# Throw-away products on TensorE in the routing's wait and ahead of three pairs of heads, and the number of expert rounds found ahead of the gates

## The chip, the cores and the metric

One core of one Trainium2 chip runs the whole program. The metric is the device time of one execution in microseconds (us). TensorE is called PE below, VectorE DVE, ScalarE ACT, GpSimd POOL and SyncE SP. SP and POOL issue the transfers (DMAs) from the chip's memory (HBM).

## What is computed

Two model blocks are run one after the other on 256 tokens of width 1024. The first block has a retention mixer, a recurrent mixer and two feed-forward networks. The second has a state-space mixer in both directions of time with a Fourier mixer beside it, and then a mixture of experts. The change touches two places in the second block.

```python
# state-space mixer, one pass (forward or backward): 16 heads, chunks of 128 tokens
seg    = where(lower, a_lr[..., :, None] - a_lr[..., None, :], -inf)
cb     = einsum('bclgn,bcsgn->bcgls', cm, bm)
y_diag = einsum('bcgrls,bcsgrp->bclgrp', cb[:, :, :, None] * exp(seg), xd)
y_off  = einsum('bcqgn,bcgrpn->bcqgrp', cm, h_in) * exp(a_cs)[..., None]
...
# hierarchical mixture of experts: 4 groups of 8 experts, the 2 best of the best group
p_grp = softmax(t @ w_rg + b_rg);  p_top_grp, grp = top_k(p_grp, 1)
p_exp = softmax(logit_sel);        p_top, j_top = top_k(p_exp, 2)
gate  = p_top_grp * p_top / sum(p_top)
y     = sum over a token's two experts of gate * ((silu(x @ w_eg) * (x @ w_eu)) @ w_ed)
```

## The kernel before

The program is one instruction stream for each engine, written by hand, with semaphores between them. An engine works strictly in the order of its stream, so a wait holds everything behind it.

**Weights.** They come from HBM in units of 128 partitions x 4096 numbers (2 MB) into six ring slots. SP issues the loads and waits for a slot to be released by PE (`slot_used`). The expert weights are 96 units, six for each pair of experts (gate, up and down, two halves each), so 16 pairs are worked off one after the other. Half of a gate unit of pairs 1, 10 and 13 is loaded into other tiles ("held": `cst`, `act2`, `lr2`, `spare`, `SQ`, `HM`, `work`), each when the tile has become free. The last held parts go into the first columns of `work`, where the routing keeps its scratch data (line 531 and the two `hold` calls behind it): SP waits there, and the loads of all later expert units are behind this wait in SP's stream.

**Heads of the state-space mixer.** The 16 heads are done in eight pairs. `head_order()` gives PE's order: for pair i first a `cb` product where a new group of four heads begins, then the `row` products of heads 2i+4 and 2i+5 (two pairs ahead), then `y`, the pair itself. Every `cb`, `row` and `y` result is a tile in one of six PSUM banks taken in turn (`ROT`), so a tile waits with `await_room` until the tile six places before it has been read. By this turn `y` of pair 1 takes the bank of row 4, `y` of pair 3 that of row 8, and `y` of pair 7 that of `y` 4. For each head h ACT reads `row` h (four activations into `HM`, or on odd heads DVE clamps it there), takes an exponential of the row into `act2` (this is the read that frees the bank) and one of `HM`, DVE multiplies `HM` with the masked `cb` (`m_ready`), and POOL multiplies `act2` with C (`ce_ready`). `y` of pair i waits for both of its heads. The tiles `HM` have four places, so head h waits for `y` of pair h/2-2. DVE also does `y_out` of each pair. After pair 7 comes the output product `mix_out`, whose last release lets SP load further expert units.

PE's stream at a pair:

```python
t = TILE["y", i]
await_room(pe, t)
...
pe.wait_ge(s["m_ready"], 2 * i + 2)
pe.wait_ge(s["ce_ready"], 2 * i + 2)
```

**Routing.** PE forms logits and turns the tokens; DVE picks group and experts in many small instructions and writes the selection `msk`. PE waits for it, counts each token's place in its expert's list (tile `route` 1, with `upper` and `ones`), counts the experts' totals into the bank `STAT` (`count_full`), and then gathers the tokens of the first experts (`gather`, 32 products into `xg` by way of ACT). DVE meanwhile makes positions, the selection `S2`, the low parts of the tokens (`token_rest`), the gates, and last the number of rounds (more than one round is needed only when an expert has over 64 tokens). `route_ready` tells all engines that the number stands in `rounds`; PE, ACT and DVE then load it into a register and enter the expert loop. `sel_ready` follows when DVE has made `SGb`, its last use of the routing's scratch.

Of the kernel before, what the change touches and what calls it, by code (L numbers as in the profile page):

```python
# [35 lines left out]
ALU = mybir.AluOpType  # L36
# [3 lines left out]
P = 128  # L40
T = 256
# [25 lines left out]
NE = NG * NJ  # L67
KE = FE // P
CAP = 64
# [156 lines left out]
def two_blocks(nc, a, out):  # L226

    ctx = ExitStack()
    with ctx:
# [242 lines left out]
        @block.sync  # L472
        def _(sp):
            sp.dma_start(vec[:, :], a["vec"]).then_inc(s["ld_vec"], 16)
            for j, piece in enumerate(("x", "w", "x", "w", "x", "x", "w", "w")):
                if piece == "x":
                    n = (0, None, 1, None, 2, 3)[j]
                    sp.dma_start(X[:, 2 * n:2 * n + 2, :], a["x"][:, 2 * n:2 * n + 2, :]).then_inc(x_in[n], 16)
                else:
                    n = (None, 0, None, 1, None, None, 2, 3)[j]  # L480
                    part = slice(n * CHUNK, (n + 1) * CHUNK)
                    sp.dma_start(ring[0][:, part], a["dense"][0][:, part]).then_inc(first_in[n], 16)
            for u in range(1, DENSE):
                if TURN[u]:
                    sp.wait_ge(slot_used[SLOT[u]], TURN[u])
                if u == DENSE - 1:
                    await_full(sp, TILE["state", SG_ - 1])
                sp.dma_start(ring[SLOT[u]][:, :], a["dense"][u]).then_inc(slot_full[SLOT[u]], 16)

            def load_expert(n, unit):  # L490
                i = EXPERT_SLOT[n]
                sp.dma_start(ring[i][:, :], a["experts"][bass.ds(unit, 1)].rearrange("u p n -> (u p) n")).then_inc(
                    slot_full[i], 16)

            def slot_free(k, r, turn):

                back = r * ring_uses(k) + turn
                sp.wait_ge(slot_used[EXPERT_SLOT[k]], back + (DENSE_USES[EXPERT_SLOT[k]] + (k == LAST_PLACE)))

            def expert_rest(r):  # L500
                with sp.Fori(0, EXPERT_UNITS // RING - 2) as b:
                    for k in range(RING):
                        slot_free(k, r, b + 1)
                        load_expert(k, b * RING + k + RING + HELD)
                for k in range(RING - HELD):
                    slot_free(k, r, EXPERT_UNITS // RING - 1)
                    load_expert(k, EXPERT_UNITS - RING + k + HELD)

            def hold(n, x, first):
                part = a["experts"][RING + n][:, first * FE:first * FE + x.shape[1]]  # L510
                sp.dma_start(x, part).then_inc(held_in[n], 16)

            hold(1, spare[:, :], 0)
            for n in range(RING):
                if EXPERT_SLOT[n] == PART_SLOT:
                    sp.wait_ge(s["h_ready"], KD)
                    first = 0
                    for x in (flat_cst, act2[:, :, :].rearrange("p a b -> p (a b)"), lr2[:, :, :].rearrange("p a b -> p (a b)")):
                        part = a["experts"][RING][:, first:first + x.shape[1]]
                        sp.dma_start(x, part).then_inc(held_in[0], 16)  # L520
                        first += x.shape[1]
                    sp.wait_ge(s["chunk_used"], CHUNKS)
                else:
                    if EXPERT_SLOT[n] == FOUR_SLOT:
                        sp.wait_ge(s["chunk_used"], MIX0 + FG)
                    sp.wait_ge(slot_used[EXPERT_SLOT[n]], DENSE_USES[EXPERT_SLOT[n]])
                load_expert(n, n)
            sp.wait_ge(s["rtok_full"], 2)
            hold(2, flat_sq[:, 0:4 * FE], 0)
            hold(2, flat_hm[:, 2 * FE:4 * FE], 4)  # L530
            sp.wait_ge(s["route_ready"], 1)
            hold(2, work[:, 0:2 * FE], 6)
            hold(1, work[:, 2 * FE:4 * FE], 6)
            expert_rest(0)
            n_rounds = sp.value_load(rounds[0:1, 0:1], min_val=1, max_val=T // CAP)
            with sp.If(n_rounds > 1):
                with sp.Fori(1, n_rounds) as r:
                    for n in range(RING):
                        slot_free(n, r, 0)
                        load_expert(n, n)  # L540
                    expert_rest(r)
            for j in range(4):
                sp.wait_ge(s["last_dve"], j + 1)
                sp.dma_start(out[:, 2 * j:2 * j + 2, :], H[:, 2 * j:2 * j + 2, :]).then_inc(s["out_done"], 16)
            sp.wait_ge(s["out_done"], 64)
# [72 lines left out]
        def _(pe):  # L618
# [285 lines left out]
            mod_rows(10)  # L904
            mod_rows(11)

            def release(name, i):
                left.append(slot_used[SLOT[UNIT_AT[name, i]]])

# [167 lines left out]
            for kind, i in head_order():  # L1077
# [10 lines left out]
                elif kind == "row":  # L1088
                    t = TILE["row", i]
                    await_room(pe, t)  # L1090
                    for d in range(2):
                        n = d * SH + i
                        one = one_of[:, n:n + 1].to_broadcast([ND, P])
                        mm(bank(t)[:, d * T:(d + 1) * T], one, a_hi[:, :], True, False)
                        mm(bank(t)[:, d * T:(d + 1) * T], one, a_lo[:, :], False, True,
                           bank_full[t % ROT] if d == 1 else None)
                else:
                    t = TILE["y", i]
                    await_room(pe, t)
                    if i == 0:  # L1100
                        pe.wait_ge(s["xd_ready"], 4)
                        await_read(pe, TILE["state", 2])
                        await_read(pe, TILE["state", 3])
                    pe.wait_ge(s["m_ready"], 2 * i + 2)
                    pe.wait_ge(s["ce_ready"], 2 * i + 2)
                    for part in range(6):
                        for h in (2 * i, 2 * i + 1):
                            rows, lo = slice(h % 2 * SP_, (h % 2 + 1) * SP_), h % 4 * SP_
                            head = slice(h * SP_, (h + 1) * SP_)
                            dm, state_of = decm[:, h % 4, :], h0[:, h // 4, :]  # L1110
                            x, cols, y = (
                                (xf[:, 0, head], slice(0, T), dm[:, 0:T]),
                                (xb[:, 0, head], slice(0, P), dm[:, T:T + P]),
                                (xf[:, 1, head], slice(P, T), dm[:, 384:384 + P]),
                                (xb[:, 1, head], slice(0, T), dm[:, 384 + P:768]),
                                (state_of[:, lo:lo + SP_], slice(0, T), ce_at[h % 4][:, 0:T]),
                                (state_of[:, 256 + lo:256 + lo + SP_], slice(0, T), ce_at[h % 4][:, T:2 * T]))[part]
                            mm(bank(t)[rows, cols], x, y, part == 0, part == 5,
                               bank_full[t % ROT] if part == 5 and h % 2 else None)
                    if i % 2 and i > 1:  # L1120
                        y_sums(i // 2 - 1)
# [54 lines left out]
                    turned(tt, [X[:, 4 * half + c, tau * P:(tau + 1) * P] for c in range(4)])  # L1176
            t = TILE["route", 1]
            await_room(pe, t)
            pe.wait_ge(s["msk_ready"], 1)
            mm(bank(t)[:, 0:NE], upper[:, :], msk[:, 0, :], True, True)  # L1180
            mm(bank(t)[:, NE:2 * NE], ones[:, :], msk[:, 0, :], True, False)
# [671 lines left out]
        def _(dve):  # L1853
# [617 lines left out]
            tt(cut(S2[:, 0, :, :].rearrange("p a b -> p (a b)"), 8, CAP), iota8, whole(posP, 0), EQ, s["eq_ready"])  # L2471
            token_rest(2)
            token_rest(3)
            dve.wait_ge(s["exp_ready"], 2)
            settle(reduce(r2(12), r2n(1, NG), ADD))
            settle(ts(r2(15), r2(14), 1.0, ADD))
# [7 lines left out]
                i = tt(cut(gw[:, tau, :], NG, NJ), og[:, tau, :].unsqueeze(2).to_broadcast([P, NG, NJ]),  # L2484
                       r2n(21, NJ)[:, tau:tau + 1, :].to_broadcast([P, NG, NJ]), MUL)
            settle(i)
            dve.wait_ge(s["count_full"], 1)
            settle(reduce(rt[:, 22, 0:1], ps[:, STAT, T:T + NE], MAX))
            for tau in range(2):
                i = ts(gP[:, tau], cut(gw[:, tau, :], NE // 4, 4), 1.0, MUL)  # L2490
            settle(i)
            ts(posP[:, NE // 4, :], posP[:, 0, :], float(CAP), SUB)
            settle(dve.tensor_copy(gateP[:, NE // 4, :], gateP[:, 0, :]))
            settle(ts(rt[:, 22, 1:2], rt[:, 22, 0:1], float(CAP), ALU.is_gt, 1.0, ADD))
            for n in range(2, T // CAP):
                settle(stt(rt[:, 22, 1:2], rt[:, 22, 0:1], float(CAP * n), rt[:, 22, 1:2], ALU.is_gt, ADD))
            dve.tensor_copy(rounds[:, 0:1], rt[:, 22, 1:2]).then_inc(s["route_ready"], 1)
            dve.wait_ge(s["route_ready"], 1)
            ts(rt[:, 23, 0:1], rt[:, 22, 0:1], 1.0, MUL, inc=s["moe_init"])
            dve.wait_ge(s["eq_ready"], 1)  # L2500
            tt(cut(SGb[:, 0, :, :].rearrange("p a b -> p (a b)"), 8, CAP),
               cut(S2[:, 0, :, :].rearrange("p a b -> p (a b)"), 8, CAP).bitcast(F32), whole(gateP, 0), MUL, s["sel_ready"])
# [224 lines left out]
```

## Time and profile before

| | |
|---|---|
| median of 3 runs | 1483.33 us (1483.03 to 1485.86) |
| the profiled execution | 1487.35 us, of which span of instructions 1485.6 us |
| PE busy | 1419.5 us (96%) |
| DVE busy | 821.1 us (55%) |
| ACT busy | 622.1 us (42%) |
| mean granted TensorE clock | 0.990 |
| transfers | 383.22 MB |

The span is the time from the first to the last instruction; 1.75 us of the profiled execution lie around it. A busy PE isn't PE at its peak, since its instructions overlap. A granted clock of 1.00 is 2.4 GHz, one of 0.50 is 1.2 GHz. In the last third of the span the transfers are nearly always busy.

### The profile page before, as it was taken

Reading aid. Unit: us, or ns where it says so; the run is one execution under the profiler, and the core shown is the slowest. Engines: PE = TensorE matmul, PEld = TensorE weight load, DVE = VectorE, ACT = ScalarE, POOL = GpSimd, SP = SyncE. Lnnn points to the kernel's source line nnn. Section 1 sums busy time; section 2 is a strip of 40 time slices with the busy share of each in tenths; the row PEclk is TensorE's granted clock in tenths of the full one; section 3 lists DMA queues with packets and bytes.
Section 4 is the critical chain, followed back from the end, with each engine's and each line's share of the span. In section 5 each row is a group of like instructions: output and inputs, shape, how many; then the busy total and the mean of one; then the engine's idle time right before and its main releaser. Section 6 shows DMA issues by size and latency. Waiting matters only on the chain.

```text
span 1485.6 us, 23733 instructions
## 1 busy us (share of the span) xinstructions
PE 1419.5 (96%) x9884; PEld 1122.0 (76%) x9884; DVE 821.1 (55%) x1216; ACT 622.1 (42%) x899; POOL 85.0 (6%) x65
## 2 busy tenths in 40 slices
PE   7999999999999999999999999798999999999997
PEld 7989799999989888999999998596434443434434
DVE  5557847776468578777458886954222222222223
ACT  6554345443456656545456665643111111111112
POOL 2000000000003102020010001500000000000000
PEclk9999999999999999999999999899999999999999
DMA  9654347445574566445561051247999999999994
GB/s 378 237 199 170 114 171 312 170 171 193 203 285 171 225 251 260 171 170 186 202 240 63 32 227 38 119 164 311 419 422 427 428 429 427 429 427 427 428 427 194
DMA packets 29041, 383.22 MB, mean 258 GB/s; under 512 B 3296, under 2 KB 3424, under 8 KB 5776
## 3 DMA queue, kind: packets, MB, share of 16 engines
q1 hardware_dynamic: 28224, 377.71, 62.7%
q0 software_dynamic: 720, 4.11, 0.7%
q8 instruction: 74, 1.21, 0.3%
q14 instruction: 23, 0.19, 0.0%
HBM read 380.76 MB, written 1.05 MB: 257 GB/s over the span
## 4 chain that ended last, share of the span: by engine, by line
PE 75%; DVE 10%; DMA 7%; ACT 5%; issue 2%; POOL 0%; SPq 0%; DVEq 0%; ACTq 0%; POOLq 0%
PE ps L631 74%; DMA ring<-in_experts 7%; DVE w_lo L1863 3%; ACT work L1334 2%; DVE work L1875 2%; ACT w_hi L1334 1%; DVE work L1863 1%; DVE X L1875 1%; ACT HM L1334 1%; DVE HM L1863 1%; DVE act L1863 0%; ACT L1334 0%; ACT act L1334 0%; PE ps L1286 0%; DMA ring<-in_dense 0%
## 5 line engine op out<-in xcount | busy, mean ns | idle before, releaser
L1863 DVE TENSOR_TENSOR w_lo<-ring,w_hi 128x1024 fp32r<-128x1024 f32 x272 | 339.7, 1258 | 215.9 <-ACT w_hi L1334 215.6
L631 PE MATMUL ps<-in_hi,w_hi 128*128 128x256 f32 x1376 | 392.8, 285 | 14.7 <-DVE w_lo L1863 14.3
L631 PE MATMUL ps<-in_hi,w_lo 128*128 128x256 f32 x1376 | 389.2, 283 | 0.0
L631 PE MATMUL ps<-in_lo,w_hi 128*128 128x256 f32 x1376 | 388.8, 283 | 0.0
L1334 ACT ACTIVATE w_hi<-ring 128x1024 fp32r<-128x1024 f32 x272 | 286.0, 1055 | 240.0 <-PE ps L631 235.9
L631 PE MATMUL ps<-ring,work 128*64 128x512 f32 (+2 forms) x1552 | 336.1, 582 | 16.2 <-ACT work L1334 12.4
L631 PEld LDWEIGHTS ps<-in_hi,w_hi 128*128 128x128 f32 x1376 | 261.7, 190 | 19.6 <-issue 16.9
L631 PEld LDWEIGHTS ps<-ring,work 128*64 128x64 f32 (+1 forms) x1552 | 113.0, 138 | 216.1 <-issue 195.8
L631 PEld LDWEIGHTS ps<-in_lo,w_hi 128*128 128x128 f32 x1376 | 261.8, 190 | 0.2
L631 PEld LDWEIGHTS ps<-in_hi,w_lo 128*128 128x128 f32 x1376 | 261.7, 190 | 0.0
L1334 ACT ACTIVATE work<-ps 128x512 f32<-128x512 f32 x64 | 37.7, 594 | 316.5 <-PE ps L1286 193.1
L1875 DVE SCALAR_TENSOR_TENSOR X<-ps,mod,X 128x256 f32<-128x256 f32 x136 | 56.8, 478 | 90.2 <-PE ps L631 89.3
L1875 DVE SCALAR_TENSOR_TENSOR yp_lo<-ps,small,yp_hi 128x512 fp32r<-128x512 f32 (+1 forms) x34 | 24.4, 719 | 147.9 <-ACT yp_hi L1334 146.5
L631 PE MATMUL ps<-hid_hi,w_hi 128*128 128x256 f32 x352 | 99.3, 282 | 0.0
L631 PE MATMUL ps<-hid_hi,w_lo 128*128 128x256 f32 x352 | 99.3, 282 | 0.0
L631 PE MATMUL ps<-hid_lo,w_hi 128*128 128x256 f32 x352 | 99.1, 282 | 0.0
L1863 DVE TENSOR_TENSOR work<-work,ps 128x512 f32<-128x512 f32 x24 | 16.1, 684 | 105.1 <-PE ps L631 105.1
L631 PEld LDWEIGHTS ps<-hid_lo,w_hi 128*128 128x128 f32 x352 | 66.7, 189 | 0.0
L631 PEld LDWEIGHTS ps<-hid_hi,w_hi 128*128 128x128 f32 x352 | 66.7, 189 | 0.0
L631 PEld LDWEIGHTS ps<-hid_hi,w_lo 128*128 128x128 f32 x352 | 66.7, 189 | 0.0
L1334 ACT ACTIVATE yp_hi<-ps,small 128x512 fp32r<-128x512 f32 (+1 forms) x34 | 22.5, 662 | 77.7 <-PE ps L631 77.7
L1875 DVE SCALAR_TENSOR_TENSOR work<-ps,vec,work 128x254 f32<-128x254 f32 (+3 forms) x80 | 44.7, 585 | 11.8 <-ACT work L1334 10.4
(283 smaller groups left out, 2053.6 us busy)
## 6 DMA issues: line engine op xcount, KB each, us to landing
ring<-in_experts SPq DMA_DIRECT2D x93, 2048.0 KB, 20.5
ring<-in_dense SPq DMA_DIRECT2D x82, 2048.0 KB, 8.5
ring<-in_dense SPq DMA_DIRECT2D x4, 512.0 KB, 7.5
spare<-in_experts SPq DMA_DIRECT2D x1, 1536.0 KB, 11.4
cst<-in_ret_cst POOLq DMA_DIRECT2D x1, 1280.0 KB, 13.1
cst<-in_experts SPq DMA_DIRECT2D x1, 1280.0 KB, 11.1
X<-in_x SPq DMA_DIRECT2D x4, 256.0 KB, 6.5
cst<-in_ctx POOLq DMA_DIRECT2D x1, 1024.0 KB, 7.8
```

What stands on the lines that cost most here:

```text
L631: i = pe.matmul(o, l, r, start=start, stop=stop)
L1334: x = act.activation(o, i, f, **kw)
L1863: i = dve.tensor_tensor(out=o, in0=x, in1=y, op=op)
L1875: i = dve.scalar_tensor_tensor(out=o, in0=x, scalar=sc, in1=y, op0=op0, op1=op1)
```

## The change

`keep_clock(n)` issues n products of `ones` with `ones` (128x128 numbers, fp32) into a bank that nobody reads. PE does 6 of them ahead of pair 1, 9 ahead of pair 3 and 8 ahead of pair 7, behind `await_room` and ahead of the waits for `m_ready` and `ce_ready`; and 16 ahead of the wait for `msk` in the routing. DVE finds the number of rounds directly behind `token_rest(3)`, ahead of the gates. SP waits for `sel_ready` where it waited for `route_ready`.

```diff
@@ block.sync
             hold(2, flat_hm[:, 2 * FE:4 * FE], 4)
-            sp.wait_ge(s["route_ready"], 1)
+            sp.wait_ge(s["sel_ready"], 1)
             hold(2, work[:, 0:2 * FE], 6)
             hold(1, work[:, 2 * FE:4 * FE], 6)
             expert_rest(0)
@@ block.tensor
+            def keep_clock(n):
+
+                for _ in range(n):
+                    pe.matmul(ps[:, MODB, 0:P], ones[:, :], ones[:, :], start=True, stop=True)
+
...
                         await_read(pe, TILE["state", 2])
                         await_read(pe, TILE["state", 3])
+                    keep_clock({1: 6, 3: 9, 7: 8}.get(i, 0))
                     pe.wait_ge(s["m_ready"], 2 * i + 2)
                     pe.wait_ge(s["ce_ready"], 2 * i + 2)
...
             t = TILE["route", 1]
             await_room(pe, t)
+            keep_clock(16)
             pe.wait_ge(s["msk_ready"], 1)
@@ block.vector
             token_rest(2)
             token_rest(3)
+            dve.wait_ge(s["count_full"], 1)
+            settle(reduce(rt[:, 22, 0:1], ps[:, STAT, T:T + NE], MAX))
+            settle(ts(rt[:, 22, 1:2], rt[:, 22, 0:1], float(CAP), ALU.is_gt, 1.0, ADD))
+            for n in range(2, T // CAP):
+                settle(stt(rt[:, 22, 1:2], rt[:, 22, 0:1], float(CAP * n), rt[:, 22, 1:2], ALU.is_gt, ADD))
+            dve.tensor_copy(rounds[:, 0:1], rt[:, 22, 1:2]).then_inc(s["route_ready"], 1)
+            dve.wait_ge(s["route_ready"], 1)
+            ts(rt[:, 23, 0:1], rt[:, 22, 0:1], 1.0, MUL, inc=s["moe_init"])
             dve.wait_ge(s["exp_ready"], 2)
             settle(reduce(r2(12), r2n(1, NG), ADD))
...
             settle(i)
-            dve.wait_ge(s["count_full"], 1)
-            settle(reduce(rt[:, 22, 0:1], ps[:, STAT, T:T + NE], MAX))
             for tau in range(2):
                 i = ts(gP[:, tau], cut(gw[:, tau, :], NE // 4, 4), 1.0, MUL)
             settle(i)
             ts(posP[:, NE // 4, :], posP[:, 0, :], float(CAP), SUB)
             settle(dve.tensor_copy(gateP[:, NE // 4, :], gateP[:, 0, :]))
-            settle(ts(rt[:, 22, 1:2], rt[:, 22, 0:1], float(CAP), ALU.is_gt, 1.0, ADD))
-            for n in range(2, T // CAP):
-                settle(stt(rt[:, 22, 1:2], rt[:, 22, 0:1], float(CAP * n), rt[:, 22, 1:2], ALU.is_gt, ADD))
-            dve.tensor_copy(rounds[:, 0:1], rt[:, 22, 1:2]).then_inc(s["route_ready"], 1)
-            dve.wait_ge(s["route_ready"], 1)
-            ts(rt[:, 23, 0:1], rt[:, 22, 0:1], 1.0, MUL, inc=s["moe_init"])
             dve.wait_ge(s["eq_ready"], 1)
             tt(cut(SGb[:, 0, :, :].rearrange("p a b -> p (a b)"), 8, CAP),
```

## Rows read from the trace of the kernel before

**Rows 1.** The stretches; columns: length, busy time by engine, granted clock, DMA share, GB/s
```profile
1005.00:1011.00 6.00, 5.84 (x51) 5.73 (x50) 1.34 (x4) 0.93 (x2) 2.03 (x2) 1.00 0.00 0
...
1084.00:1460.00 376.00, 355.16 (x1802) 152.99 (x1800) 91.32 (x189) 60.24 (x107) 0.00 (x0) 1.00 1.01 428
```

**Rows 2.** Waits of PE's weight loads from 1060 to 1466 us
```profile
PEld ps L631 <- DMA ring<-in_experts: 7.6, 9, 2.1
```

**Rows 3.** The chain that ended last
```profile
990.49 19.27 PE ps L631 x160
```

**Rows 4.** Timeline of PE, heads: start, time, [idle before <-releaser]
```profile
931.98 2.41 PE L631 MATMUL ps<-HM,work 128*64 128x256 f32 x16 [1.73 <-ACT act L1334]
...
935.98 0.38 PE L631 MATMUL ps<-a_hi,pick 32*128 32x256 f32 x1
...
944.02 2.83 PE L631 MATMUL ps<-HM,work 128*64 128x256 f32 x16 [2.33 <-ACT act L1334]
...
948.49 1.62 PE L631 MATMUL ps<-work,ones 128*128 128x256 f32 x4
...
965.92 2.23 PE L631 MATMUL ps<-HM,work 128*64 128x256 f32 x16 [2.18 <-DVE HM L1863]
```

**Rows 5.** Timeline of ACT, heads
```profile
931.30 0.62 ACT L1334 ACTIVATE act<-ps 128x512 f32<-128x512 f32 x1
...
943.36 0.61 ACT L1334 ACTIVATE act<-ps 128x512 f32<-128x512 f32 x1
...
948.66 1.35 ACT L1334 ACTIVATE HM<-ps,small 128x256 f32<-128x256 f32 x4 [2.36 <-PE ps L631]
```

**Rows 6.** Timeline of DVE, heads
```profile
930.91 0.97 DVE L1863 TENSOR_TENSOR HM<-HM,work 128x768 f32<-128x768 f32 x1
...
938.75 1.41 DVE L1863 TENSOR_TENSOR HM<-HM,work 128x768 f32<-128x768 f32 x1 [1.00 <-ACT HM L1334]
...
942.56 0.94 DVE L1863 TENSOR_TENSOR HM<-HM,work 128x768 f32<-128x768 f32 x1
...
954.67 1.15 DVE L1863 TENSOR_TENSOR work<-ps,cst 128x256 f32<-128x256 f32 x4 [0.59 <-PE ps L631]
```

**Rows 7.** Stretches of PE's clock; columns as in rows 1
```profile
932.50:935.80 3.30, 3.30 (x22) 2.09 (x18) 3.27 (x7) 1.48 (x3) 2.05 (x2) 0.50 1.06 451
...
942.70:949.40 6.70, 5.38 (x26) 3.39 (x27) 6.06 (x10) 4.07 (x10) 2.90 (x2) 0.50 0.01 2
...
966.60:969.90 3.30, 3.30 (x21) 2.05 (x17) 0.07 (x2) 0.31 (x1) 0.00 (x0) 0.50 0.02 5
...
1017.80:1024.60 6.80, 5.11 (x23) 5.04 (x24) 6.03 (x23) 0.92 (x3) 0.00 (x0) 0.50 1.03 419
```

**Rows 8.** Timeline of PE, routing
```profile
1012.98 1.95 PE L775 MATMUL ps<-ident,X 128*128 128x128 f32 x16
1018.91 0.61 PE L631 MATMUL ps<-work,upper 128*128 128x32 f32 x2 [3.99 <-DVE work L1863]
1019.33 0.61 PE L631 MATMUL ps<-work,ones 128*128 128x32 f32 x2
...
1021.80 0.55 PE L631 MATMUL ps<-S,t_hi 128*128 128x256 f32 x1 [0.58 <-DVE S L1863]
...
1027.85 2.37 PE L631 MATMUL ps<-ring,work 128*64 128x512 f32 x10 [0.77 <-ACT work L1334]
```

**Rows 9.** Timeline of DVE and SP, routing
```profile
1020.41 0.22 DVE L1875 SCALAR_TENSOR_TENSOR work<-ps,work 128x64 f32<-128x64 f32 x1 [0.32 <-PE ps L631]
...
1026.38 1.73 SPq L511 DMA_DIRECT2D work<-in_experts  x2
...
1026.46 0.68 DVE L1863 TENSOR_TENSOR work<-S,work 128x512 f32<-128x512 f32 x1
```

**Rows 10.** Stretches of the early expert loop; columns as in rows 1
```profile
1068.00:1072.00 4.00, 4.00 (x30) 2.69 (x26) 1.35 (x3) 0.00 (x0) 0.00 (x0) 1.00 0.97 336
...
1080.00:1084.00 4.00, 4.00 (x21) 1.35 (x19) 2.70 (x4) 0.66 (x1) 0.00 (x0) 1.00 0.91 373
```

## Prediction

> **What bounds the kernel now.** I read the page first, then the busy time by stretch, the waits, the chain that ended last, and last the timelines of the two places that the change touches.
>
> From 1011 us on the transfers are the bound. In the 376 us from 1084 the DMA share is 1.01 and 428 GB/s flow throughout; in the six microseconds ahead of 1011 nothing is moved [rows 1]. So a stream that can't go faster starts at 1011, and what ends the kernel is its start, plus its bytes, plus whatever it stands still on the way, plus PE's tail behind the last units. PE is close behind: its weight loads wait for expert units nine times, 7.6 us in all [rows 2]. That is the slack by which PE could be late, and it says that making PE alone earlier in this part is worth nothing at the end. What starts the stream is the last release behind `mix_out`, and `mix_out` is PE's own work up to there [rows 3]. So time won or lost in the heads moves the stream's start one for one, and time won in the routing does not.
>
> **The heads.** Ahead of pairs 1, 3 and 7 PE stands idle for 1.73, 2.33 and 2.18 us [rows 4], and behind each of the three the granted clock is 0.50, which is 1.2 GHz, for 3.3, 6.7 and 3.3 us [rows 7]. A pair at that clock takes 4.5 us (944.02 to 948.49, [rows 4]), so 2.2 to 2.4 at 1.00.
>
> The question is what ended each idle time, for the added products stand behind the bank's wait and ahead of the heads' wait. Pair 1 takes the bank of row 4. ACT's read of that row ends at 931.30 + 0.62 = 931.92 [rows 5], DVE's product of head 3 ends at 930.91 + 0.97 = 931.88 [rows 6], and PE starts at 931.98. The two waits end together, so the added products have no idle time to lie in. Pair 3 takes the bank of row 8, read until 943.36 + 0.61 = 943.97 [rows 5], while head 7 is ready at 942.56 + 0.94 = 943.50 [rows 6]: here the bank alone ends the wait, and PE starts at 944.02 [rows 4]. Pair 7 takes the bank of pair 4, read long before; it waits for DVE [rows 4]. Only there can the products fill the wait.
>
> The price of one product is not in the trace as such. One instruction with 128 columns of weights and 128 of data takes 1.95 / 16 = 0.12 us at full clock, and the two of an fp32 product are 1019.33 - 1018.91 = 0.42 us at half clock [rows 8], hence 0.21 to 0.24 at full. I take 0.22 and 0.42. That nothing later on PE overtakes them no run here shows: the Trainium skill, "TensorE: Matmul & The Clock Gate", Part 3, states that products start and end strictly in program order.
>
> *Pair 1.* Six products cost 1.3 us at full and 2.5 at half clock. The clock falls half a microsecond behind 931.98 [rows 7], since the idle time that took it away lies before the products: two at full, four at half, 2.2 us. The pair then starts at 934.2, runs at half until 935.9, does the remaining six tenths at full in 1.4 and ends at 937.3. Before, the next product started at 935.98 [rows 4]. That is +1.3. ACT and DVE were waiting for this pair (DVE sat idle for 1.00 us at 938.75, behind ACT, [rows 6]), so all of it goes on.
>
> *Pair 3.* The bank comes free at 943.97 + 1.3 = 945.3, nine products at full clock take 2.0, the pair 2.4: end at 949.7 against 948.49, +1.2. At half clock throughout it would be 3.8 + 4.5, end at 953.6, +5.1. PE's idle time ahead of the nine is longer than before, so I let the half clock hold for part of it and take +1.8. ACT waits directly for this end (2.36 us at 948.66, [rows 5]). Further on DVE had 0.59 us of idle time at 954.67 [rows 6] that swallows its part: +1.2 is left.
>
> *Pair 7.* Eight products take 1.8 us and fit into 2.18. The clock holds, and the 3.3 us at half [rows 7] become 1.65: -1.6. Bounds: nothing if the clock falls all the same, -1.6.
>
> Heads together: +1.2 - 1.6 = -0.4 us at the start of the stream.
>
> **The routing.** PE is idle for 3.99 us [rows 8]. Its 16 products need 3.5 and fit; the bank they stand behind is free by then. The half clock from 1017.8 to 1024.6 [rows 7] would go. The counting ends sooner, which takes away DVE's 0.32 us wait [rows 9]; the gathers, which start at 1021.80 [rows 8] and ran at half until 1024.6, save 1.4 more. The loop's first product at 1027.85 [rows 8] could come 1.7 us earlier, if the number of rounds is there. It is: DVE wrote it at about 1026.3 (SP, released by it, issues at 1026.38, [rows 9]), and it now comes ahead of some twenty small instructions of the gates. DVE's total is unchanged.
>
> On the stream this has two effects. SP now waits for the end of `SGb`, 1026.46 + 0.68 = 1027.14, less 0.32, so it issues at 1026.83 instead of 1026.38 [rows 9]: +0.45. Queued behind the wait are both held parts and every later expert unit. Whether it costs depends on what is still under way; nothing to +0.45, and I take all of it. Against that, the stream stands partly still twice early in the loop, at 336 and 373 GB/s in 4 us each [rows 10], because PE's releases come late: against 428 GB/s that is 0.86 + 0.51 = 1.4 us. Releases 1.7 us earlier win back nothing to 1.4; I take 1.0.
>
> **Sum.** -0.4 + 0.45 - 1.0 = -0.95 us on the profiled execution's 1487.35, so 1486.4. That execution lies 4.02 us above the median of the runs; on the median, 1483.33 - 0.95 = 1482.4 us. Within 0.2%, 3 us, is about what can't be told from no change here.
>
> **The rivals.**
>
> *A, faster: the added products lie in the waits.* If the bank of pairs 1 and 3 came free earlier than in this one execution, nothing is delayed and all three pairs run at full clock. DVE's idle 1.00 and 0.59 [rows 6] and up to 1.5 of ACT's 2.36 [rows 5] go, and 1.6 at pair 7: -4.7 + 0.45 - 1.0 = -5.2, 1478.1 us. Against it: both banks are freed by ACT's own order of work, not by anything that varies. It decides once pair 3's `y` ends before 947.
>
> *B: PE, not the stream, sets the end in undisturbed executions.* The profiled one is 4 us slower than the median; if that is transfers, PE's 7.6 us of waits [rows 2] are mostly gone, and the routing's 1.7 counts instead of the stream's terms: -0.4 - 1.7 = -2.1, 1481.2 us.
>
> *C, slower: the nine products ahead of pair 3.* They start only when the bank is free, at half clock: +5.1, less 0.59, less 1.6, is +2.9; with +0.45 and nothing won back +3.4, 1486.7 us. For it: PE's idle time there grows. Against: the clock was full for all PE did from 935.9 to the fall before 942.7 [rows 7]. It decides once pair 3 ends over 4.7 us later than before.
>
> *D, slower: products of `ones` don't hold the clock.* Then all cost and nothing is won: 2.5 at pair 1; at pair 3 2.5 + 3.8 + 4.5 from 943.97, end 954.8, +6.3, less 0.59; at pair 7 3.4 us in a wait of 2.18, +1.2; with 0.45 it is +7.4, 1490.7 us. The Trainium skill, same page, Part 1, states of another limiter of this clock, that of the peak current, that it depends on the data and isn't tripped by all-ones operands; of the gate it says only that it watches how busy PE is. No row here shows a product of constants.
>
> **How the numbers follow.** My sum 0.50, A 0.14, B 0.17, C 0.13, D 0.06. The likeliest gives 1482.4, with a range of its own from 1480.5 to 1484.8. The range of 8 in 10 reaches to A below and nearly to C above: 1478.0 to 1486.5. Faster by over 0.2%: A, and the lower edges of B and of my sum, 0.25. Slower: C, most of it, and D, 0.17. The same: 0.58.
>
> **What would show it.** Behind `await_room` of pair 1 the first product of `ones` starts at 931.9 and `y` 1 2.2 us later; if `y` 1 starts at 932.0, my reading of the bank falls, and with it the sign in the heads. `y` 3 should start about 3 us later than before and end 1 to 2 later; `y` 7 should run at 1.00 in 2.4 us. In the routing the clock should stay at 1.00 and the loop's first product come 1.7 us closer to `msk`. The stream's start, the SP issue behind `mix_out`, should be within 1 us of 1011; if the end moves otherwise than this start less what the two thin stretches give back, the stream isn't the bound. The prediction is most easily wrong by the clock: its falls are all-or-nothing, and one fall more or less is 1.6 us.

## Result and the profile after

The changed kernel takes 1486.9 us (median of 20 runs, 1483.65 to 1489.9), the kernel before 1485.16 us (20 runs, 1483.03 to 1488.28). The ratio is 1.0015, with a 95% interval from 1.0008 to 1.0021 (it is not the quotient of the two medians, which is 1.0012 or 1.7 us): slower by about 2.2 us, which is less than the 0.2% that I had called the bound of what can be told here, and yet clear of zero. Forecast was 1482.4 us, 0.95 us faster than the median shown, with a range up to 1486.5. The profiled execution took 1487.77 us, only 0.42 more than that of before; why the two profiles show less than the medians is told under "The base" below. All ratios here are of runs in the fast state; of all runs one was not in it (1769.41 us, products at pairs 1 and 7) and is left out.

The page of the kernel after, its first lines:

```profile
span 1486.0 us, 23888 instructions
...
PE 1423.6 (96%) x9962; PEld 1126.3 (76%) x9962; DVE 822.2 (55%) x1216; ACT 622.5 (42%) x899; POOL 85.7 (6%) x65
```

The totals tell little, so I go to the two places. The timeline of PE in the heads, after; columns as in rows 4:

```profile
925.08 1.30 PE L631 MATMUL ps<-HM,work 128*64 128x256 f32 x13
...
931.60 2.33 PE L910 MATMUL ps<-ones 128*128 128x128 f32 x12 [1.74 <-ACT act L1341]
933.86 2.41 PE L631 MATMUL ps<-HM,work 128*64 128x256 f32 x16
...
937.06 0.38 PE L631 MATMUL ps<-a_hi,pick 32*128 32x256 f32 x1
...
945.12 3.49 PE L910 MATMUL ps<-ones 128*128 128x128 f32 x18 [2.35 <-ACT act L1341]
948.55 1.90 PE L631 MATMUL ps<-HM,work 128*64 128x256 f32 x16
...
951.24 1.13 PE L631 MATMUL ps<-work,ones 128*128 128x256 f32 x4
...
959.30 2.58 PE L631 MATMUL ps<-HM,work 128*64 128x256 f32 x16 [1.28 <-ACT act L1341]
...
963.30 1.13 PE L631 MATMUL ps<-work,ones 128*128 128x256 f32 x4
...
966.67 2.05 PE L910 MATMUL ps<-ones 128*128 128x128 f32 x16
969.83 1.52 PE L631 MATMUL ps<-HM,work 128*64 128x256 f32 x16 [1.10 <-DVE HM L1870]
...
972.14 1.13 PE L631 MATMUL ps<-cst,ones 128*128 128x256 f32 x4
```

The same view of the kernel before, only what rows 4 don't have:

```profile
925.45 1.31 PE L631 MATMUL ps<-HM,work 128*64 128x256 f32 x14
...
956.78 1.52 PE L631 MATMUL ps<-HM,work 128*64 128x256 f32 x16 [1.03 <-ACT act L1334]
...
959.10 1.13 PE L631 MATMUL ps<-work,ones 128*128 128x256 f32 x4
...
969.78 1.22 PE L631 MATMUL ps<-cst,ones 128*128 128x256 f32 x4
```

The first row of each is the start of pair 0, the last point that the change can't reach. Counted from it (us), by these rows and [rows 4]:

| event | before | after | later by |
|---|---|---|---|
| PE goes on ahead of pair 1 | 6.53 | 6.52 | 0 |
| pair 1 has ended (next product) | 10.53 | 11.98 | 1.45 |
| PE goes on ahead of pair 3 | 18.57 | 20.04 | 1.47 |
| pair 3 has ended | 23.04 | 26.16 | 3.12 |
| pair 5 starts | 31.33 | 34.22 | 2.89 |
| pair 5 has ended | 33.65 | 38.22 | 4.57 |
| pair 7 starts | 40.47 | 44.75 | 4.28 |
| pair 7 has ended | 44.33 | 47.06 | 2.73 |
| the stream of expert units starts | 85.71 | 88.36 | 2.65 |

The last line of the table is SP's first issue behind `mix_out`, here in the timeline of SP, before:

```profile
1011.16 0.33 SPq L492 DMA_DIRECT2D ring<-in_experts  x1
...
1032.56 10.25 SPq L492 DMA_DIRECT2D ring<-in_experts  x4
```

and after, with the held parts behind the wait for `sel_ready`:

```profile
1013.44 0.33 SPq L492 DMA_DIRECT2D ring<-in_experts  x1
...
1029.04 0.80 SPq L511 DMA_DIRECT2D work<-in_experts  x2
1033.86 10.24 SPq L492 DMA_DIRECT2D ring<-in_experts  x4
```

The stretches after, the first four in the heads, the next two in the routing, the last two the thin ones of [rows 10]; columns as in rows 1:

```profile
932.40:935.60 3.20, 3.20 (x20) 2.60 (x20) 3.17 (x6) 1.33 (x2) 1.78 (x2) 0.50 1.04 444
946.00:949.30 3.30, 3.30 (x17) 2.85 (x17) 3.27 (x4) 1.33 (x2) 2.05 (x2) 0.50 0.00 0
959.70:962.90 3.20, 3.20 (x22) 2.11 (x20) 3.17 (x6) 1.61 (x3) 2.39 (x2) 0.50 0.00 0
966.60:969.90 3.30, 2.20 (x20) 1.94 (x20) 3.27 (x5) 1.61 (x3) 2.02 (x2) 1.00 0.00 0
1017.10:1020.70 3.60, 3.60 (x33) 3.48 (x32) 3.08 (x20) 2.90 (x6) 0.00 (x0) 1.00 0.95 404
1024.50:1027.80 3.30, 3.30 (x17) 3.30 (x17) 2.82 (x18) 2.01 (x4) 0.00 (x0) 0.50 1.07 448
1068.00:1072.00 4.00, 4.00 (x26) 2.05 (x23) 1.32 (x3) 0.00 (x0) 0.00 (x0) 1.00 1.03 430
1080.00:1084.00 4.00, 4.00 (x20) 1.34 (x18) 2.63 (x4) 1.38 (x2) 0.00 (x0) 1.00 0.99 401
```

And PE in the routing after; columns as in rows 8:

```profile
1017.03 3.74 PE L910 MATMUL ps<-ones 128*128 128x128 f32 x32
1021.10 0.41 PE L631 MATMUL ps<-work,upper 128*128 128x32 f32 x2 [0.33 <-DVE work L1870]
...
1023.67 0.36 PE L631 MATMUL ps<-S,t_hi 128*128 128x256 f32 x1 [1.26 <-DVE S L1870]
...
1029.15 2.37 PE L631 MATMUL ps<-ring,work 128*64 128x512 f32 x10
```

What the reader is to see: the loss is in the heads and arrives at the stream whole (2.73 at pair 7, 2.65 at the stream's start). The products ahead of pairs 1 and 3 start only when ACT has freed the bank, behind the same idle time as before (1.74 and 2.35 us against 1.73 and 2.33, [rows 4]), and the clock falls to 0.50 in both places all the same, now among the products. A third half-clock stretch, at pair 5, stands where before's trace has none. Pair 7 and the products ahead of it run at 1.00. In the routing the clock holds through the 16 products and the counting, then falls in the middle of the gathers, behind 1.26 us in which PE waits for DVE's `S`. From the stream's start to the last landing of an expert unit it was 455.1 us before and 453.3 after (1466.30 - 1011.16 and 1466.73 - 1013.44): the routing gives 1.9 us back. On the trace's own clock the start is 2.28 later, so the span is 0.4 longer.

### The profile page after: what moved, and what is told of

It is laid out like the page before. It is cut to its first block, busy times and chain, and to the rows that moved or that the text cites. A ratio compares the mean times of both kernels' runs of the same rounds, so it can differ in the third digit from the quotient of the medians.

```text
span 1486.0 us, 23888 instructions
## 1 busy us (share of the span) xinstructions
PE 1423.6 (96%) x9962; PEld 1126.3 (76%) x9962; DVE 822.2 (55%) x1216; ACT 622.5 (42%) x899; POOL 85.7 (6%) x65
## 4 chain that ended last, share of the span: by engine, by line
PE 75%; DVE 11%; ACT 6%; DMA 6%; issue 2%; SPq 0%; POOL 0%; DVEq 0%; ACTq 0%; POOLq 0%
PE ps L631 73%; DMA ring<-in_experts 5%; DVE w_lo L1870 3%; ACT work L1341 2%; DVE work L1882 2%; ACT HM L1341 1%; DVE work L1870 1%; ACT w_hi L1341 1%; DVE X L1882 1%; DVE HM L1870 1%; DMA ring<-in_dense 1%; DVE in_lo L1882 0%; DVE act L1870 0%; ACT act L1341 0%; ACT L1341 0%
```

## The experiments

Each kernel was timed in five rounds against the kernel before on the same chip. "Start" below is the stream's start behind pair 0, as in the table (before 85.71, after 88.36); it and the number of half-clock stretches in the heads come from one profiled execution each, and such an execution can lie up to 2.7 us from its kernel's median (1482.91 for 1485.6 with products at pairs 1 and 7, 1492.34 for 1489.79 at pairs 1 and 3). The number of runs is 11 or 12, but 6 for pairs 1 and 3 and 7 for the last experiment.

### The change in two halves

**Heads' products alone**: the kernel before, with `keep_clock` as in the change at the three pairs, nothing in the routing.

```diff
+                    keep_clock({1: 6, 3: 9, 7: 8}.get(i, 0))
                     pe.wait_ge(s["m_ready"], 2 * i + 2)
```

> The kernel before with the added products of the heads alone (6, 9 and 8, behind the bank's wait); routing and SP's wait as before. Theory 'bank': the 15 products ahead of pairs 1 and 3 start only when the bank is free and delay them; SP's issue behind mix_out comes 2 to 3 us later than before (before: 1011.2), the time is 1.5 to 3 us above that of before. Rival 'routing': the heads' products lie in idle time and SP's later wait is what costs; the issue comes at 1011 or earlier and the time is that of before or 1 to 2 us below.

Measured: 1488.71 against 1484.85 us, ratio 1.0024 (1.0013 to 1.0035). Start 87.99, falls at pairs 1, 3 and 5 as in the changed kernel.

**Routing's part alone**: the changed kernel without the heads' products.

```diff
-                    keep_clock({1: 6, 3: 9, 7: 8}.get(i, 0))
```

> The changed kernel without the heads' products: 16 products in the routing's wait, the earlier number of rounds and SP's wait for sel_ready are left. Theory 'bank': the stream starts where it did before and gets back at most what the early loop stood still; time 0 to 1.5 us below before. Rival 'routing': SP's later issue of the held parts holds the stream; time 1 to 2.5 us above before.

Measured: 1483.26 against 1484.85 us, ratio 0.9985 (0.9975 to 0.9996). The two halves add up to +0.09%, which agrees with the change's +0.15% within their intervals. So the heads lose about 3.6 us (0.24%) and the routing wins about 2.2 (0.15%).

### Which pair

All of these are the kernel before with `keep_clock` behind the bank's wait at some of the pairs; the diff is one line, and only the table in it differs.

**Pair 7 alone**

```diff
+                    keep_clock({7: 8}.get(i, 0))
```

> The kernel before with the 8 products ahead of pair 7 alone, where PE waits for DVE and not for a bank. Theory 'bank': y of pair 7 runs at 1.00 in 2.4 us instead of 3.9, the stream starts 1 to 1.6 us earlier, and so does the end. Rival: the clock falls elsewhere or mix_out takes the gain up; time within 0.5 us of before.

Measured: 0.9998 (0.9989 to 1.0006), start 82.03. Pair 7 ran at 1.00; the 1 to 1.6 us expected don't show in the time.

**Pair 3 alone**

```diff
+                    keep_clock({3: 9}.get(i, 0))
```

> The kernel before with the 9 products ahead of pair 3 alone, behind the bank's wait. Theory 'bank': they start at about 944 and y of pair 3 starts 2 to 4 us later; the time is 1 to 3 us above before. If instead pair 1 is what costs, this one is within 0.5 us of before.

Measured: 1.0000 (0.9989 to 1.0012), start 84.36. In that execution the nine products ran at full clock (942.3 to 944.6): a fall at pair 2 (937.2) had made PE late, so that it had no idle time ahead of them and the bank was free. It says nothing of what the nine cost where PE waits for the bank.

**Pair 1 alone**

```diff
+                    keep_clock({1: 6}.get(i, 0))
```

> The kernel before with the 6 products ahead of pair 1 alone, behind the bank's wait. Theory 'bank': pair 1 ends 1 to 2 us later and its followers wait for it; the time is 0.5 to 2.5 us above before. With pair 3 alone at 1.000 and pair 7 alone at 0.9998 of before, pair 1 would have to carry most of the 0.24% of the three together, or their costs add up only together.

Measured: 0.9998 (0.9988 to 1.0008), start 86.21.

No pair alone costs anything that can be measured, against what I had expected of pairs 3 and 1. So the pairs two at a time:

**Pairs 1 and 3**

```diff
+                    keep_clock({1: 6, 3: 9}.get(i, 0))
```

> The kernel before with the products ahead of pairs 1 and 3, behind the bank's wait; none at pair 7. Each of the three places alone measured within 0.1% of before, all three together 1.0024. Theory 'the delays add and pair 5 then falls': pair 1's delay carries pair 3 with it, and in both traces with all three pair 5 ran at 0.50 as well; time 2 to 4 us above before, stream start at 1012 or later. Rival 'chip and clock phase': the 1.0024 came from the phase of the clock in that call; this one is within 1 us of before.

Measured: 1489.79 against 1484.5 us, ratio 1.0033 (1.0021 to 1.0045), the slowest of all; start 90.89. Its profiled execution was the slowest of its six runs, 2.6 us above their median. The timeline of PE of this kernel, pairs 1, 3, 5 and 7:

```profile
933.03 2.93 PE L910 MATMUL ps<-ones 128*128 128x128 f32 x12 [1.74 <-ACT act L1340]
935.89 2.83 PE L631 MATMUL ps<-HM,work 128*64 128x256 f32 x16
...
947.72 2.96 PE L910 MATMUL ps<-ones 128*128 128x128 f32 x18 [2.35 <-ACT act L1340]
950.61 2.44 PE L631 MATMUL ps<-HM,work 128*64 128x256 f32 x16
...
961.90 2.04 PE L631 MATMUL ps<-HM,work 128*64 128x256 f32 x16 [1.29 <-ACT act L1340]
...
972.14 2.03 PE L631 MATMUL ps<-HM,work 128*64 128x256 f32 x16 [2.84 <-DVE HM L1869]
```

and its stretches at those places:

```profile
932.20:935.50 3.30, 2.47 (x11) 2.47 (x12) 3.30 (x7) 2.61 (x5) 1.70 (x2) 0.50 1.03 436
935.60:938.80 3.20, 3.20 (x20) 2.16 (x21) 1.90 (x2) 0.13 (x1) 0.75 (x1) 0.50 1.02 435
949.20:952.40 3.20, 3.20 (x22) 2.60 (x22) 2.88 (x4) 0.80 (x2) 1.61 (x1) 0.50 0.00 0
962.90:966.10 3.20, 3.20 (x15) 1.69 (x12) 3.17 (x4) 1.68 (x3) 1.81 (x2) 0.50 0.00 0
973.10:976.30 3.20, 3.20 (x16) 1.95 (x13) 0.38 (x1) 0.04 (x1) 0.00 (x0) 0.50 0.00 0
```

All four odd pairs have a half-clock stretch here, the first one twice as long as usual.

**Pairs 3 and 7**

```diff
+                    keep_clock({3: 9, 7: 8}.get(i, 0))
```

> The kernel before with the products ahead of pairs 3 and 7, behind the bank's wait. If pair 1 is needed for the loss, within 1 us of before; if any two add up, 1 to 3 us above.

Measured: 1.0009 (0.9998 to 1.0021), start 82.62.

**Pairs 1 and 7**

```diff
+                    keep_clock({1: 6, 7: 8}.get(i, 0))
```

> The kernel before with the products ahead of pairs 1 and 7. If pairs 1 and 3 together make the loss, within 1 us of before, since neither alone costs more; if any two add up, 1 to 3 us above.

Measured: 1.0000 (0.9987 to 1.0013), start 83.11.

What follows: the only kernels with a loss clear of zero are the ones with products at pairs 1 and 3 together. Pair 3 with pair 7 is the least sure of the others, with an interval up to 1.0021. With pair 7 added to 1 and 3 the loss shrinks from 0.33% to 0.24%, 1.3 us, about what was forecast for pair 7, though the intervals of the two overlap.

### The place of the products

**Ahead of the bank's wait**: the changed kernel with the heads' products three lines earlier. The same products in the same number, but they can run in the idle time, since they don't touch the bank that is waited for.

```diff
+                    keep_clock({1: 6, 3: 9, 7: 8}.get(i, 0))
                     t = TILE["y", i]
                     await_room(pe, t)
...
-                    keep_clock({1: 6, 3: 9, 7: 8}.get(i, 0))
                     pe.wait_ge(s["m_ready"], 2 * i + 2)
```

> The changed kernel with the heads' products moved ahead of the bank's wait, all else kept. Theory 'bank': the products now lie in PE's idle time, y of pair 1 starts when the bank is free (about 931.6 by this clock, not 933.9), y of pair 3 too, the clock holds at more of the pairs, SP's issue behind mix_out comes 1 to 4 us earlier than before and the time falls by as much. Rival 'routing': no difference to the changed kernel, 1 to 2.5 us above before. Rival 'clock': the products don't hold the clock wherever they stand; pairs 1 and 3 still run at 0.50, time that of before.

Measured: 1481.91 against 1484.85 us, ratio 0.9979 (0.9969 to 0.9989); start 80.85. The timeline of PE of this kernel:

```profile
931.10 1.60 PE L910 MATMUL ps<-ones 128*128 128x128 f32 x12
932.91 1.52 PE L631 MATMUL ps<-HM,work 128*64 128x256 f32 x16 [0.20 <-ACT act L1341]
...
941.98 2.27 PE L910 MATMUL ps<-ones 128*128 128x128 f32 x18
944.18 1.52 PE L631 MATMUL ps<-HM,work 128*64 128x256 f32 x16
```

and its stretch over both pairs:

```profile
931.00:947.00 16.00, 14.76 (x126) 11.36 (x125) 15.90 (x33) 12.46 (x27) 9.00 (x7) 1.00 0.56 235
```

Pair 0 began at 926.38 here, so pair 1 starts 6.53 us behind it, exactly as before the change, and pair 3 starts 17.80 behind it instead of 18.57. The clock is 1.00 throughout the heads. The same edit turns from a loss into a gain by where the line stands. So it is the place behind the bank's wait that makes the heads' products a loss; how the loss then grows is another matter, and partly open (see the end of the next section).

What this kernel still wastes stands in its routing. The clock fell at 1008.4, ahead of it, so the 16 products ran partly at half clock:

```profile
1013.11 4.73 PE L910 MATMUL ps<-ones 128*128 128x128 f32 x32
1017.68 0.31 PE L631 MATMUL ps<-work,upper 128*128 128x32 f32 x2
```

In DVE's timeline the selection `msk` is written by 1015.46, while the counting starts at 1017.68, and DVE stands idle for 1.69 us waiting for it: here the products outlasted the wait that they were to fill, and held the counting up by 2.2 us. In the changed kernel they took 3.74 us and the counting still waited 0.33 for DVE.

**The same without the routing's part**: the kernel before with the heads' products ahead of the bank's wait, by the added line of the diff above.

> The kernel before with the heads' products alone, ahead of the bank's wait. Theory 'bank': 0 to 3 us below before, where the same products behind the wait were 3.6 us above it.

Measured: 0.9991 (0.9980 to 1.0001), start 82.34, one fall (at 952.9, pair 5). By the time alone this isn't separated from no change; from the 1.0024 (1.0013 to 1.0035) of the same products behind the wait it is.

### The routing

**Order alone**: the changed kernel without any products, so the number of rounds ahead of the gates and SP's wait for `sel_ready`.

```diff
-                    keep_clock({1: 6, 3: 9, 7: 8}.get(i, 0))
...
-            keep_clock(16)
```

> The changed kernel without any throw-away products: the number of rounds ahead of the gates and SP's wait for sel_ready alone. If the order is what brings the routing's gain, about 2 us below before as with the routing's part whole; if it is the clock of the counting and the gathers, 0 to 0.5 us below or above before, since the gathers still run at 0.50 and end when they did.

Measured: 0.9997 (0.9986 to 1.0008). The clock fell in the routing as before (1015.4 to 1022.2). The intervals of this and of 0.9985 overlap, so the times don't tell whether the 16 products or the order bring the gain. The profiles give most of it to the order. In the timeline of PE of this kernel the loop's first product is

```profile
1024.45 4.08 PE L631 MATMUL ps<-ring,work 128*64 128x512 f32 x18
```

which is 15.98 us behind the stream's start and has no idle time ahead of it. Before, it stood 16.69 behind, and PE was idle for 0.77 us ahead of it [rows 8], though the gathers started at the same time (10.64 in both) and ran at half clock in both. Only that idle time is gone, with the number of rounds found early. The 16 products bring the loop from 15.98 to 15.71.

**SP's wait alone**

```diff
-            sp.wait_ge(s["route_ready"], 1)
+            sp.wait_ge(s["sel_ready"], 1)
             hold(2, work[:, 0:2 * FE], 6)
```

> The kernel before with SP waiting for sel_ready instead of route_ready, nothing else. My sum put +0.45 us on it as an upper bound: the held parts are issued at about 1027.2 instead of 1026.4. The theory that the stream has no slack there expects up to +0.8 us; the rival that enough is still under way expects 0.

Measured: 1.0002 (0.9992 to 1.0013). The wait for `sel_ready` costs nothing that can be measured.

**A later loop**: the kernel before with nine products between the gathers and the loop.

```diff
                 gather(0, half, GATHER0[half])
+            keep_clock(9)
             pe.wait_ge(s["route_ready"], 1)
```

> The kernel before with 9 throw-away products between the gathers and the expert loop: PE's loop starts about 2 us later, nothing else moves. 'Stream alone bounds': PE's slack takes it up, 0 to 0.5 us. 'The first release bounds the stream': the first expert unit behind the held parts is issued 2 us later, the stream stands still for 1 to 2 us there, and the time rises by 1 to 2 us.

Measured: 1.0005 (0.9994 to 1.0017). The loop came only 1.2 us later, at 17.87 us behind the stream's start for 16.69, since the products also filled PE's 0.77 us of idle time there. A loss as large as these 1.2 us (0.08%) lies inside the interval, and so does none: the time doesn't decide.

The profiles say more here than the times. Counted from the stream's start, they show when the loop's first product comes, what the transfers carry in the first 100 us, and how long the stream lasts until its last landing:

| executions | loop at, us | GB/s, first 100 us | stream, us |
|---|---|---|---|
| after, routing's part alone | 15.71, 15.71 | 417, 418 | 453.3, 453.0 |
| order alone | 15.98 | 416 | 453.6 |
| before and ten others | 16.53 to 16.75 | 410 to 413 | 453.9 to 456.3 |
| pair 3 alone | 17.20 | 410 | 456.7 |
| late loop | 17.87 | 407 | 456.8 |

From 100 to 400 us all sixteen carry 428 GB/s. So the loop's start sets how much is lost early in the stream, though PE waits for units later on: a loop 1 us earlier gives 5 GB/s over 100 us, about 1.2 us of stream at 428 GB/s. The rest of the stream's length comes beyond 400 us and varies by itself: among the eleven executions with the loop in one place it differs by 2.4 us. In the two versions with all products ahead of the banks' waits the loop is at 16.55 and 16.59, because of the late counting told above; those kernels are fast by their heads.

**Four more products between counting and gathers**, on top of the version with all products ahead of the banks' waits:

```diff
                 mm(ps[:, STAT, T:T + NE], ones[:, :], msk[:, 1, :], False, True, s["count_full"])
+            keep_clock(4)
```

> The changed kernel with the heads' products ahead of the bank's wait, and 4 more products between the counting and the gathers, where PE stood idle for about 1.3 us in the changed kernel and the clock fell during the gathers. If the clock holds, the gathers take 3.9 us and the loop starts up to 1.5 us earlier relative to msk: time at or up to 1 us below that kernel without the 4 (0.9979 of before). Rival: the 4 delay the gathers as the 9 delayed pair 3; time 0.5 to 1 us above it.

Measured: 1480.93 against 1485.89 us, ratio 0.9966 (0.9953 to 0.9980), the fastest of all. The timeline of PE of this kernel:

```profile
1018.29 1.14 PE L910 MATMUL ps<-ones 128*128 128x128 f32 x8
1019.44 0.36 PE L631 MATMUL ps<-S,t_hi 128*128 128x256 f32 x1
...
1023.39 1.94 PE L631 MATMUL ps<-ring,work 128*64 128x512 f32 x8
```

The four products end at 1019.43, and DVE has `S` ready at 1019.29. The gathers and all behind them run at 1.00. But in the version without them the clock also held in its profiled execution, and the two ratios were taken on different chips, with overlapping intervals: what these four bring isn't separated.

## Why the prediction was wrong

**How far off.** The forecast was 1482.4 us and 1486.9 were measured, 4.5 more. Of these 1.8 are the base: I had taken the median of three runs, 1483.33, and that of twenty is 1485.16. The other 2.7 are the change, forecast at -0.95 and measured at +1.7 between the medians.

**The bound, and the way from heads to stream: right.** The stream started 2.65 us later for 2.73 at pair 7. PE still waits for expert units eight times, 7.0 us in all (nine times and 7.6 before, [rows 2]).

**Pair 1: right.** Forecast +1.3, measured +1.45. The products stood behind ACT's read, started at the same time as PE had gone on before, and the clock fell among them. That products start and end strictly in program order the Trainium skill states ("TensorE: Matmul & The Clock Gate", Part 3); the trace agrees: pair 3 starts at 948.55, just as the products' 3.49 us from 945.12 are over.

**Pair 3: the mechanism right, the price wrong.** This is the first failed term of the step "Heads together". I let the half clock hold for part and took +1.8 at the end of the pair, with the nine products at 2.0 us. They took 3.43 (945.12 to 948.55), all but the first 0.8 us of them at 0.50, and the pair 2.69 (to 951.24): 6.12 against the 4.47 of the pair alone before [rows 4], +1.65, and with the 1.47 from pair 1 it is +3.12. The idle time ahead of the products was the same as before, 2.35 for 2.33 us, and not longer, as I had said; and the clock fell a second time. I had the half-clock price of the products (0.42 each) and used it for pair 1 only. It was too low besides: I had read it off products of 32 columns [rows 8]. Wholly at 0.50 six of them took 2.86 us in the kernel with pairs 1 and 3 (933.03 to 935.89), 0.48 each.

**What swallows it: wrong.** I had DVE's 0.59 us [rows 6] take its part. The delay shrank by 0.23 up to pair 5's start.

**Pair 5: a term that isn't in the sum.** Its clock fell, behind 1.28 us of idle time; before, 1.03 us stood there and no fall followed. The pair took 4.00 us instead of 2.32, +1.68. Pair 7's heads wait for pair 5 by the four places of `HM`, so 4.28 of the 4.57 reached pair 7. The fall at this place stands in all three executions that had products behind the waits at both pair 1 and pair 3, and in none of the five that had them at one of the two at most. But a fall at pair 5 stands also in the execution of SP's wait alone (954.8), whose heads are those of before, and in that of the heads' products ahead of the bank alone (952.9), which delay nothing. Nor is it the length of the idle time: with all products ahead of the bank PE was idle for 1.27 us there (954.54), and the clock held. Why the clock falls there in one case and not in another no run tells.

**Pair 7: right.** Forecast -1.6, measured 4.28 - 2.73 = -1.55; the stretch that was at 0.50 [rows 7] is at 1.00. With the eight products the clock held at pair 7 in all eight profiled executions that had them; without them it fell there in five of eight. So the 1.6 us are not there to be won each time, and timed alone pair 7 brought nothing that can be measured (0.9989 to 1.0006).

The heads' sum by measured terms: 1.45 + 1.67 - 0.23 + 1.68 - 0.29 - 1.55 = +2.7, where I had -0.4. That failed step alone turns the sign.

**The routing: right in sign, too small, and for another reason than mine.** Forecast was +0.45 for SP's wait and -1.0 won back, -0.55 in all. Timed by itself, the part brings -2.2 us, with an interval from -3.7 to -0.6. SP's issue came 0.38 later behind the stream's start (15.60 for 15.22), as forecast; its cost can't be measured (1.0002, from 0.9992 to 1.0013), and 0.45 us can't be told from nothing either. The loop's first product came only 0.9 closer to `msk` (8.05 us for 8.94) and not 1.7, since the clock fell again in the gathers. And most of this 0.9 isn't the clock's: order alone brings 0.7 (8.23), by the 0.77 us in which PE stood idle ahead of the loop [rows 8] and which my sum didn't have. That the sign came out right is in part luck. The ring's next issue stands 20.42 behind the start for 21.40, and the two thin stretches carry 430 and 401 GB/s for 336 and 373 [rows 10]. The stream took 1.9 less. Of these about 1.2 are won in its first 100 us (417 GB/s for 412), which is inside my bound of 1.4 for the two stretches; the rest comes beyond 400 us, where the executions differ by themselves.

**The base.** I added terms from one execution to the median of runs. Five executions with the heads as before (the kernel before, the routing's part alone, order alone, SP's wait alone, the later loop) have three, three, one, two and two half-clock stretches there, and their starts are 85.71, 86.72, 81.84, 82.48 and 83.73: mean 84.1. So the profiled execution before was a poor one, 1.6 above this mean and in its time 2.2 above the median of twenty (1487.35 for 1485.16; that of after only 0.9 above its own), and the falls that the products should cure aren't there each time, while their cost behind the bank's wait is. The two executions with all products behind the wait lie at 88.2, which is 4.1 later and fits the 3.6 timed; the three with them ahead of it at 80.9, 80.9 and 82.3.

**The rivals.** A (the products lie in the waits) falls, since the banks came free as late as I had read; moved ahead of the wait they do lie there. B falls in its mechanism (PE still waits for units), though the routing's gain is nearer to its 1.7 than to my 0.55. C gave 1486.7 us, near the 1486.9 measured, but by a pair 3 that ends over 4.7 us later; it ended 3.12 later, and the rest is pair 5. Half of C happened. D falls: products of `ones` hold the clock at 1.00, over 3.6 us ahead of the counting and through it, where it was 0.50 before [rows 7], and at pair 7. What the Trainium skill states in "TensorE: Matmul & The Clock Gate", Part 1, of all-ones operands is of another limiter; for the fall of the clock that this case shows, constants count as work (at pair 7, eight executions of eight against three of eight without them).

**What stays open.** Why pairs 1 and 3 cost 0.33% together and nothing each alone. All three executions with both had the fall at pair 5, and starts of 88.0 to 90.9; those with one at most lie at 82.0 to 86.2, as without any products (81.8 to 86.7). My guess is that one delay moves a later fall away about as often as it brings one; one profile each doesn't show it.

## What to carry to other kernels

Filler work that is to keep an engine's clock up must stand ahead of the wait that makes the idle time: find which wait ends last (here a PSUM bank read by ACT, not the operands), since behind it each filler is a plain delay, at half clock and at twice its price. It must not outlast that wait either: sixteen products that fitted at full clock held the counting up by 2.2 us where the clock had fallen. Price filler by the clock that is granted there, and follow the delay to the next idle time on the engine, which may bring a fall of its own. When the clock's falls differ from execution to execution, take several profiles before you book a fall as something to be won.

## What the runs showed that I had not expected

- Where the clock falls differs between executions of the same work: the same heads had one to three half-clock stretches, and the stream's start moved by 4.9 us with them (81.84 to 86.72).
- The clock fell behind idle times as short as 1.28 us (pair 5) and 1.26 us (gathers). Idle times of about the same length (1.03 ahead of pair 5 before, 1.27 there and 0.99 ahead of the gathers in the version ahead of the bank) were followed by none.
- Fp32 products of 128x128 by 128 columns took 0.24 us each at full clock (nine in 2.20) and 0.48 at half (six in 2.86).
- How much the stream loses in its first 100 us depends on when PE enters the loop, although PE waits for its units later on: 416 to 418 GB/s with the loop at 15.7 to 16.0 us behind the stream's start, 410 to 413 at 16.5 to 16.8, 407 at 17.9.
- The loop had waited for the number of rounds: finding it earlier took 0.77 us of idle time of PE away, without any product.
